# Order of work in an NSA, MLA and mixture-of-experts trunk on one core: VectorE's maxima ahead of its scaling, compressed transposes half a unit later, expert 0 behind chunk 0

## The reference

```python
for i in range(2):
    h = rmsnorm(x, norm_mix[i])
    mix = nsa_mixer(h, ...) if i == 0 else mla_mixer(h, ...)
    x = x + mix
    h = rmsnorm(x, norm_ffn[i])
    x = x + hier_moe(h, ...)
```

## Time and profile before

| | us |
|---|---|
| median of 3 runs | 1909.38 |
| lowest and highest | 1902.38, 1917.9 |
| the profiled execution | 1915.49 |
| its span in the profile | 1913.7 |
| PE busy | 1489.8 (78%) |
| DVE busy | 600.8 (31%) |
| ACT busy | 314.1 (16%) |
| POOL busy | 234.1 (12%) |
| HBM, mean over the span | 257 GB/s |

### The profile page before, as it was taken

The page is one execution under the profiler, slowest core; times in us unless marked ns, Lnnn a source line. Parts: engine busy times, 40 slices in busy tenths (PEclk is TensorE's granted clock), DMA queues, the critical chain, the costliest instruction groups (busy, mean ns, idle before and its releaser), DMA issues. The chain is left out here.

```text
span 1913.7 us, 24152 instructions
## 1 busy us (share of the span) xinstructions
PE 1489.8 (78%) x8891; PEld 849.6 (44%) x8891; DVE 600.8 (31%) x1528; ACT 314.1 (16%) x890; POOL 234.1 (12%) x276
## 2 busy tenths in 40 slices
PE   7999888889687777777765678779687777777772
PEld 3644455545443443443333456555353343334431
DVE  2144565534511111111114254543521111111113
ACT  2112355530100000000001122221110000000000
POOL 1111000000211111111113000000111111111112
PEclk9999899999799999999997798979899999999997
DMA  5122010031399999999974300000569999999994
GB/s 216 61 89 88 1 67 1 1 157 75 117 413 427 430 425 421 421 417 419 424 320 143 154 1 0 0 0 23 232 279 429 429 420 423 419 415 421 416 422 171
DMA packets 39410, 468.08 MB, mean 245 GB/s; under 512 B 11680, under 2 KB 12192, under 8 KB 21568
## 3 DMA queue, kind: packets, MB, share of 16 engines
q1 hardware_dynamic: 22288, 434.76, 54.3%
q0 software_dynamic: 15776, 27.93, 4.2%
q10 hardware_dynamic: 1296, 4.72, 0.6%
HBM read 452.66 MB, written 39.85 MB: 257 GB/s over the span
## 5 line engine op out<-in xcount | busy, mean ns | idle before, releaser
L1008 PE MATMUL ps<-sb_ring,sb_x_block 128*64 128x256 f32 x4096 | 471.2, 383 | 173.1 <-DMA sb_ring<-moe_w 166.8
L1008 PEld LDWEIGHTS ps<-sb_ring,sb_x_block 128*64 128x64 f32 x4096 | 311.0, 137 | 384.6 <-issue 145.6
L1017 PE MATMUL ps<-sb_ring,sb_hidT 128*64 128x512 f32 x1024 | 248.0, 605 | 45.5 <-ACT sb_hidT L753 45.5
L1667 DVE COPY sb_row_now<-sb_row_of 128x1 uint32 (+1 forms) x128 | 19.7, 154 | 764.1 <-PE ps L1017 754.0
L660 POOL DMA_INDIRECT expert_rows<-sb_y_sb,sb_row_now x128 | 126.0, 985 | 864.5 <-DVE sb_y_sb L1668 841.7
L753 ACT COPY sb_hidT<-ps 128x128 f32<-128x128 f32 x128 | 34.1, 266 | 888.7 <-PE ps L1077 888.7
L1017 PEld LDWEIGHTS ps<-sb_ring,sb_hidT 128*64 128x64 f32 x1024 | 62.1, 136 | 143.0 <-issue 73.1
L1668 DVE COPY sb_y_sb<-ps 128x512 f32<-128x512 f32 x128 | 87.1, 680 | 0.0
L934 ACT ACTIVATE sb_ring<-ps,sb_n_max_of 128x128 f32<-128x128 f32 (+3 forms) x128 | 66.4, 524 | 73.8 <-DVE sb_n_max_of L2008 73.7
L1439 PE MATMUL ps<-sb_ring 64*128 64x128 f32 (+3 forms) x256 | 54.5, 504 | 24.5 <-ACT sb_ring L934 23.9
L1677 DVE COPY sb_x_block<-sb_xsT 128x512 f32 x132 | 56.4, 427 | 24.7 <-issue 22.7
(11 more groups left out here) (280 smaller groups left out, 1635.9 us busy)
## 6 DMA issues: line engine op xcount, KB each, us to landing
sb_ring<-moe_w SPq DMA_DIRECT2D x128, 3072.0 KB, 16.5
sb_xsT<-nsa_w_group SPq DMA_DIRECT2D x2, 2048.0 KB, 14.5
sb_ring<-nsa_w_group SPq DMA_DIRECT2D x2, 2048.0 KB, 7.6
sb_xsT<-nsa_w_out SPq DMA_DIRECT2D x1, 4096.0 KB, 13.4
token_rows<-sb_h_norm ACTq DMA_DIRECT2D x8, 512.0 KB, 2.9
sb_ring<-mla_w_out SPq DMA_DIRECT2D x1, 4096.0 KB, 13.3
sb_ring<-mla_w_in SPq DMA_DIRECT2D x1, 2304.0 KB, 8.6
sb_x_res<-x SPq DMA_DIRECT2D x4, 512.0 KB, 6.8
```

Of the source, the lines that this page charges most:

```text
L1008: last = nc.tensor.matmul(ps[j * BLOCK:(j + 1) * BLOCK, bank, 0:2 * P].rearrange("p (g n) -> p g n", g=2), x_rows[:, k, :], weights[:, 0:2 ...
L1017: last = nc.tensor.matmul(ps[j * BLOCK:(j + 1) * BLOCK, 2, :], hidT[:, c * BLOCK:(c + 1) * BLOCK], weights[:, 2, c * D + j * 512:c * D + ( ...
```

## The change

Three orders change; no instruction of the computation is added or taken away.

1. In the attention loop DVE runs top(s + 2) ahead of scale_probs(s + 1).
2. `cmp_turn` of group g moves on PE from behind unit 4g + 7 to the middle of unit 4g + 8, and `cmp_copy` on ACT from behind the work of unit 4g + 7 to ahead of that of unit 4g + 8. Group 2's have no such unit: they come after scores(1) on PE and after exps(1) on ACT. Group 3's stay.
3. In the expert stage up(0) comes behind chunk 0, down(0) behind chunk 4, down(1) behind chunk 7. Block 0 is taken once chunk 0 is copied, block 1 once chunks 0 to 4 are, blocks 2 and 3 once all are. The first two experts are written out on PE, ACT and DVE; PE's loop and ACT's now begin at expert 2, as DVE's did before.

```diff
--- before.py
+++ after.py
@@ -425,6 +425,7 @@
         UP_BANKS = (0, 3)
         OUT_BANKS = 2
         CHUNK_BANK = 4
+        FIRST = 2
         NSA_UNITS = 0
         MLA_STEPS = 16
         SCORE_BANKS = (0, 1, 4)
@@ -752,11 +753,24 @@
                     act.wait_ge(hid_turned, done + 1)
                     nc.scalar.copy(hidT[:, :], ps[:, 1, 0:P]).then_inc(hidT_ready, 1)
 
-                for c in range(CHUNKS):
+                def chunk_half(c):
                     act.wait_ge(chunk_turned, l * CHUNKS + c + 1)
                     nc.scalar.copy(xsT[:, 0:4, c * P:(c + 1) * P],
                                    ps[:, CHUNK_BANK + 2 * (c % 2), :].rearrange("p (k n) -> p k n", k=4)).then_inc(xsT_act, 1)
-                with act.Fori(0, EXPERTS // 2) as i:
+
+                chunk_half(0)
+                gate(base, 0)
+                chunk_half(1)
+                chunk_half(2)
+                turn_hidden(base)
+                chunk_half(3)
+                chunk_half(4)
+                gate(base + 1, 1)
+                chunk_half(5)
+                chunk_half(6)
+                turn_hidden(base + 1)
+                chunk_half(7)
+                with act.Fori(1, EXPERTS // 2) as i:
                     for u in range(2):
                         done = i * 2 + (base + u)
                         gate(done, u)
@@ -911,6 +925,8 @@
                     nc.scalar.copy(cmp_PT[:, g, :], ps[:, cmp_banks(g)[1], :]).then_inc(c_probsT_ready, 1)
 
                 for u in range(UNITS):
+                    if u >= 8 and u % TILES == 0:
+                        cmp_copy(u // TILES - 2)
                     unit_rows(u)
                     if u >= 1 and u - 1 < UNITS - 1:
                         unit_columns(u - 1, 0)
@@ -921,8 +937,6 @@
                         spread_values()
                     if u >= 6 and u % TILES == 2:
                         cmp_exp(u // TILES - 1)
-                    if u >= 7 and u % TILES == 3:
-                        cmp_copy(u // TILES - 1)
 
                 def exps(s):
                     n = (s % TILES + 1) * P
@@ -937,6 +951,7 @@
 
                 exps(0)
                 exps(1)
+                cmp_copy(KV_GROUPS - 2)
                 for s in range(ATTEND):
                     n = (s % TILES + 1) * P
                     act.wait_ge(n_turned, 2 * s + 2)
@@ -1096,18 +1111,31 @@
                             xs_in(c).rearrange("p (m k) -> p k m", k=KD)[:, k, :], ident[:, :])
                     last.then_inc(chunk_turned, 1)
 
-                for c in range(CHUNKS):
-                    turn_chunk(c)
+                turn_chunk(0)
                 up(0, 0, 0)
-                with pe.Fori(0, EXPERTS // SLOTS - 1) as i:
+                turn_chunk(1)
+                turn_chunk(2)
+                turn_hidden(0)
+                turn_chunk(3)
+                turn_chunk(4)
+                finish(0, 0)
+                up(1, 1, 0)
+                turn_chunk(5)
+                turn_chunk(6)
+                turn_hidden(1)
+                turn_chunk(7)
+                finish(1, 1)
+                up(FIRST, FIRST, 0)
+                turns = (EXPERTS - FIRST - 2) // SLOTS
+                with pe.Fori(0, turns) as i:
                     for u in range(SLOTS):
-                        up(i * SLOTS + (u + 1), (u + 1) % SLOTS, i + (u + 1) // SLOTS)
-                        down(i * SLOTS + u, u, i)
-                last = EXPERTS // SLOTS - 1
-                for u in range(SLOTS):
-                    if u + 1 < SLOTS:
-                        up(last * SLOTS + u + 1, u + 1, last)
-                    down(last * SLOTS + u, u, last)
+                        n = u + FIRST
+                        up(i * SLOTS + (n + 1), (n + 1) % SLOTS, i + (n + 1) // SLOTS)
+                        down(i * SLOTS + n, n % SLOTS, i + n // SLOTS)
+                for n in range(EXPERTS - 2, EXPERTS):
+                    if n + 1 < EXPERTS:
+                        up(n + 1, (n + 1) % SLOTS, (n + 1) // SLOTS)
+                    down(n, n % SLOTS, n // SLOTS)
                 s = ex[l]
                 pe.wait_ge(tables_ready, l + 1)
                 n = pe.value_load(extra_n[0:1, l:l + 1], min_val=0, max_val=MAX_EXTRA)
@@ -1410,6 +1438,8 @@
                     if u >= 2:
                         unit_columns(u - 2, 0)
                         unit_columns(u - 2, 1)
+                    if u >= 8 and u % TILES == 0:
+                        cmp_turn(u // TILES - 2)
                     unit_rows(u, range(KD // 2, KD))
                     if u == 0:
                         turn_gates()
@@ -1420,8 +1450,6 @@
                         turn_keys()
                     if u >= 6 and u % TILES == 2:
                         cmp_scores(u // TILES - 1)
-                    if u >= 7 and u % TILES == 3:
-                        cmp_turn(u // TILES - 1)
 
                 def scores(s):
                     pair, kind, t = s // PAIR_STEPS, s // TILES % 2, s % TILES
@@ -1475,6 +1503,7 @@
                 unit_columns(UNITS - 2, 0)
                 unit_columns(UNITS - 2, 1)
                 scores(1)
+                cmp_turn(KV_GROUPS - 2)
                 for s in range(ATTEND + 1):
                     if s + 2 < ATTEND:
                         scores(s + 2)
@@ -1673,29 +1702,38 @@
                     nc.vector.tensor_copy(xsT[:, 4:8, c * P:(c + 1) * P],
                                           ps[:, CHUNK_BANK + 2 * (c % 2) + 1, :].rearrange("p (k n) -> p k n", k=4)).then_inc(xsT_dve, 1)
 
+                def first_block(n, chunks):
+                    dve.wait_ge(xsT_act, l * CHUNKS + chunks)
+                    dve.wait_ge(xsT_dve, l * CHUNKS + chunks)
+                    r = dve.value_load(start_i[0:1, l, n:n + 1], min_val=0, max_val=ROWS)
+                    nc.vector.tensor_copy(x_block[:, n % 2], xsT[:, :, bass.ds(r, BLOCK)]).then_inc(block_ready, 1)
+
+                chunk_half(0)
+                first_block(0, 1)
+                dve.wait_ge(silu_done, base + 1)
+                join_hidden(0)
+                for c in range(1, 5):
+                    chunk_half(c)
+                first_block(1, 5)
+                keep_rows(0, 0)
+                dve.wait_ge(silu_done, base + 2)
+                join_hidden(1)
+                for c in range(5, CHUNKS):
+                    chunk_half(c)
+                first_block(2, CHUNKS)
+                first_block(3, CHUNKS)
+                keep_rows(0, 1)
+
                 def take_block(where, buffer):
                     return nc.vector.tensor_copy(x_block[:, buffer], xsT[:, :, bass.ds(where, BLOCK)])
 
-                for c in range(CHUNKS):
-                    chunk_half(c)
-                dve.wait_ge(xsT_act, (l + 1) * CHUNKS)
-                dve.wait_ge(xsT_dve, (l + 1) * CHUNKS)
-                for n in range(2):
-                    r = dve.value_load(start_i[0:1, l, n:n + 1], min_val=0, max_val=ROWS)
-                    take_block(r, n).then_inc(block_ready, 1)
-
-                def one_expert(i, u):
-                    dve.wait_ge(silu_done, i * 2 + (base + u + 1))
-                    join_hidden(u)
-                    r = dve.value_load(start_i[0:1, l, bass.ds(i * 2 + (u + 2), 1)], min_val=0, max_val=ROWS)
-                    take_block(r, u).then_inc(block_ready, 1)
-                    keep_rows(i, u)
-
-                for u in range(2):
-                    one_expert(0, u)
                 with dve.Fori(1, EXPERTS // 2) as i:
                     for u in range(2):
-                        one_expert(i, u)
+                        dve.wait_ge(silu_done, i * 2 + (base + u + 1))
+                        join_hidden(u)
+                        r = dve.value_load(start_i[0:1, l, bass.ds(i * 2 + (u + 2), 1)], min_val=0, max_val=ROWS)
+                        take_block(r, u).then_inc(block_ready, 1)
+                        keep_rows(i, u)
                 s = ex[l]
                 n = dve.value_load(extra_n[0:1, l:l + 1], min_val=0, max_val=MAX_EXTRA)
                 with dve.If(n > 0):
@@ -2028,10 +2066,10 @@
                 scale_probs(0)
                 unit_norm(UNITS - 1)
                 for s in range(ATTEND):
+                    if s + 2 < ATTEND:
+                        top(s + 2)
                     if s + 1 < ATTEND:
                         scale_probs(s + 1)
-                    if s + 2 < ATTEND:
-                        top(s + 2)
                     if s == 1:
                         unit_rotate(UNITS - 1)
                     if s == 9:
```

## The result

The changed kernel takes 1856.16 us (median of 4 runs, 1851.75 to 1858.53), against 1905.93 for the kernel before measured with it: a ratio of 0.9725 with a 95% interval of 0.9675 to 0.9776. Two repetitions of the changed kernel, each beside the kernel before, gave 1856.11 (ratio 0.9737, 0.9714 to 0.9760) and 1855.27 (0.9737, 0.9713 to 0.9761).

What follows compares the result with a forecast made beforehand. Attention was taken as bound by a chain through ACT and DVE, the expert stage by its weight stream. Parts 1, 2 and 3 gave 20 + 11 + 2.4 = 33 us, from 1909.4 to 1876 us, range 1862 to 1894.

Steps and rivals of the forecast that it cites:

- So PE is next, at 9.8: Attention loop: with scaling off the chain, PE's busy time, 9.8 us for four steps, is the next bound.
- Not all of the waits on it go: Attention loop: PE still waits 0.5 us a period for scaling behind tile 3's maximum, giving 10.3 us against 11.73.
- 15 x 1.9 = 28: Attention loop: upper bound in us of the maxima-first gain, where PE never waits.
- The third one decides: Expert stage, layer 0: the third weight transfer, behind down(2), leaves 3.0 us of the 8.4 gained at the head.
- down(2) at 538.0: Expert stage, layer 0: expert 2's down product ends at 538.0 us; minus 14.6 gives 523.4, against 526.4 before.
- The Trainium skill's rule: Expert stage's head: up(0) at half clock throughout, 7.2 us in place of 5.5; part 3 would give -1 us.
- (a): Attention loop: PE's hand-overs keep the period near 11.0, saving 0.7; 1886 us in all; chance 0.15.
- (b): Attention loop: another loop as long lies behind the chain, attention saves nothing; 1896 us; chance 0.07.
- (c): DVE's queue in attention: the maximum in front holds scaling, PE waits every step, 51 us price; 1947 us; chance 0.05.
- (d): Expert stage's head: chunk rows land late or blocks wait, up to 4 us lost a layer; 1886 us; chance 0.08.
- Four steps take 10.1 to 10.6: Attention loop: sign of a right forecast, four steps (tiles 0 to 3) in 10.1 to 10.6 us, against 11.73.

Runs made afterwards that it cites:

- part 1 alone: On the kernel before, only top(s + 2) moved ahead of scale_probs(s + 1) in the attention loop: 1880.31 us, ratio 0.9864.
- part 2 alone: On the kernel before, only the calls of cmp_copy and cmp_turn moved as in the change: 1894.36 us, ratio 0.9940.
- part 3 alone: The change with the first two edits taken back, so only the expert stage's head is reordered: 1903.20 us, ratio 0.9973.
- the late down(0) kernel: The changed kernel with down(0) behind up(1) in place of ahead of it: 1861.85 us, ratio 0.9765.

## Why the prediction was wrong

The sign, the order of the parts and the mechanism were right; two terms of the sum were too small, and the sum (33) fell short of 49.8. Of the 20 us between the forecast (1876) and the time (1856), 3.5 are the kernel before, whose median was 1909.4 when I forecast and 1905.9 beside the changed kernel.

- **Part 1, forecast 20, measured 34.9 us of stage time in the first pair.** Over all profiled executions the attention takes 198.1 to 200.1 us in the old order and 165.2 to 166.2 in the new one (with the mask and the new order in every step), so some 33; the whole time of part 1 alone fell by 27.7. Right: scaling left the chain, PE came next, and the wait that is left is the one for tile 2's scaling behind tile 3's maximum. The step that failed is "So PE is next, at 9.8". I divided the busy time of the earlier trace rows by eleven periods as though it were work, but the row itself says clock 0.97: a mean of 0.97 is 6% of the stretch at half clock, 7.7 us in which at most half is stretching, 3.9 us, so 108.14 - 3.9 = 104.3 us or 9.5 a period. In the new loop PE is busy 9.3 (98.84 us over 102 / 9.65 = 10.6 periods); the 0.2 between the two isn't explained. Then "Not all of the waits on it go", 0.5 a period: 0.3 came (3.2 us of 102). Together 9.6 for 10.3. And 1 us was taken off for half clock that didn't occur: the new loop runs at 1.00. Each of these errors is small, but what they are taken from is a difference: 11.73 - 9.65 = 2.1 instead of 1.4, over 16 periods rather than 15. The bound of "15 x 1.9 = 28" fell with the same 9.8.
- **Part 2, forecast 11, measured 11.4 in the first pair** (11.2 between the means of the five profiled executions with the old place and the ten with the new one), and 13.7 by the medians of part 2 alone. Right, with the wait gone and the 5.29 back at its length.
- **Part 3, forecast 2.4, measured 10.6** (5.8 + 4.8) in the first pair. Between the means of five profiled executions with the old order and six with the new one the last down products come 5.0 and 4.4 earlier; part 3 alone saved 4.8 by its median, in which the forecast's 2.4 isn't excluded (2.1 to 8.2). The step that failed is not "The third one decides" but where the third one stands, "down(2) at 538.0", which is 37.5 behind chunk 0. It came at 35.5. Two chunks take 2.05 us, not 2.5 (the price was from four chunks in one run, 5.03 us in the earlier trace rows, which probably held waits for their copies; in pairs they show none), and the hand-overs of blocks 1 and 2 are 0.17 and 0.16 us of wait, not 0.3. Up(0) was worse than I had it, 6.36 and 6.09 against 5.5. And a transfer takes 7.65 us, not 7.27, so two of them take off 15.3 and not 14.6. Together the stream starts at 20.2 us behind chunk 0 in layer 0, where I had 22.9, and at 19.4 in layer 1, where I had 22.4. The old start in layer 1 was also not the 21.8 of the one profile that I had, but 21.8 to 23.9 over five executions, 22.7 on average. From there to the last down product it takes 472.4 to 474.4 us in the ten layers with the old order and 471.9 to 473.1 in the twelve with the new one; the profile before had the longest of them in layer 1, so 2.4 of its 4.8 us are not the head, and what they are stays open.
- **The Trainium skill's rule** (TensorE: Matmul & The Clock Gate, "What's actually happening": throttled is the default, activity releases it) was weighed with up(0) at 7.2 us. It ran 6.36 and 6.09, between that and my 5.5: the trace agrees with the rule as far as the clock stayed at 0.50 through the wait and rose only 5.5 us into the product. With chunk 1 in the wait it rose before the product, which took 3.67. But none of this decided part 3.
- **The rivals.** (a), hand-overs of PE: no, PE is busy 97% of the stretch. (b), another loop as long: no. (c), the maximum holds the scaling: in six of some 42 steps, 0.5 us each, 3.2 us in 102; far less than the chain gave. (d), the head gets worse: no.

Of what was named as showing it, PE is above 92% (97%), the maximum follows its scores closely, down(0) ends 9.0 us earlier in layer 0 (5.7 in layer 1), and the DMA engines stand nearly still from 489 to 491 us, ahead of the third transfer. "Four steps take 10.1 to 10.6" was not met, exponentials still wait up to 1.7 us for a maximum, PE first waits for weights at the eighth expert and not the fifth, and expert 2's down product came 35.5 us behind chunk 0, not 37.5.

## What to carry to other kernels

When an engine is next in line as the bound, take its work, not its busy time: divide out the granted clock of the same row, because stretches at half clock may sit in waits that the change removes, and a small error in a floor is a large one in the difference. Where a chain over two engines runs through an in-order queue, put the work that is ready ahead of the work that waits, for every step; the old order in one step of four gave back 0.2 of the 2.1 us. Where PE must wait for a hand-over ahead of a product, give it any work that it has to do anyway: here 1.9 us of transposes moved into a wait of 2.7 took 2.7 us of half clock off the product behind it. And compare a stage's gain with the whole time's: parts 1 and 3 each saved some 5 us less than their stages, and why isn't shown.

## What was unexpected of the hardware

- The old loop had stretches at the lower level (1.2 GHz, as in the earlier trace rows), a mean granted clock of 0.97 over 129 us. In parts 2 and 3 alone, with the same loop, it was 0.93 and 0.97. Four more short matmuls a step, which left the loop's length as it was, kept the clock at the upper level over the same stretch; two fewer a step went with 0.95. None of this moved the attention by more than 2 us (198.1 to 200.1).
- The MLA mixer, untouched by any edit, runs at a mean granted clock of 0.88 in some executions of one and the same kernel and 0.91 in others, and of the 6.4 us between the two spans compared above (1856.7 and 1850.2) 5.1 arise between layer 0's chunk 0 and layer 1's, 4.9 of them behind the last down product of layer 0. Within one kernel the faster execution is nearly always the one with the higher granted clock: the changed kernel's four took 1858.4, 1858.5, 1853.9 and 1851.8 us at 0.950, 0.949, 0.953 and 0.955.
- A product of 32 matmuls took 3.67 us behind a wait of 0.86 us, 5.36 behind one of 2.03, and 6.36 behind one of 2.69, though other products kept 3.67 behind a wait of 2.04 (in the late down(0) kernel): the wait alone doesn't say it.
